# The adaptive modulation of a two-block kernel moved to TensorE, with its loads and those of x begun together

## The chip, the cores and the metric

One core of a Trainium2 chip runs the whole program. The metric is the device time of one execution in microseconds (us), as the median of the runs shown. All data is float32.

## The reference, cut to what matters

The function takes x (256 tokens of 1024 features) through two transformer blocks. The first one scales and shifts its normed input, and gates its branches, by six vectors that come from one vector c:

```python
mod = silu(c) @ w_ada + b_ada                        # (1, 1024) @ (1024, 6144)
sh1, sc1, g1, sh2, sc2, g2 = split(mod, 6)
u = rmsnorm(h, norm1_w) * (1.0 + sc1) + sh1
proj = u @ w_in                                      # hq, hf, hi, hg, aq, ak, av
...                                                  # gated recurrence (hgrn2) and differential attention
h = h + g1 * (mix @ w_out)
u = rmsnorm(h, norm2_w) * (1.0 + sc2) + sh2
h = h + g2 * ((silu(u @ w_gate) * (u @ w_up)) @ w_down)
```

The second block (gated linear attention, retention, a mixture of 32 experts with two per token, final norms) follows and has no part in the change.

## The kernel before, in words

Everything is one hand-scheduled program. Each engine has its own function (`tensor`, `scalar`, `vector`, `gpsimd`, `sync`) which is one long list of instructions in a fixed order; semaphores tie them together.

**Matrix products.** A product with 1024 input features and 512 output features (a `Gemm`, called hf, hq, aq, ak, av, hv, hg, wo0, ...) is cut into four units of two 128-feature chunks. The float32 weights of a unit are split into a high and a low half, ScalarE writing the high one (L846) and VectorE the low one (L1224), into a ring of three units (`WHL`). The activations are split in the same way into `XH` and `XL`. TensorE (L505) adds up three products for each chunk: high by high, low by high, high by low. A Gemm hands over control twice, after its second and after its fourth unit; such a half is called a half-product below.

**Weights.** SyncE issues all weight loads in one order into a ring of six slots of 1 MB, and waits before each until the slot is free. The modulation's matrix w_ada has twelve column blocks of 512 (ada0 to ada11), each of two loads (rows 0 to 511 and 512 to 1023). The order is ada0 to ada3, hf, hq, aq, ada4, ada5, ak, ada6, ada7, av, ada8, ada9, hv, hg, wo0, wo1, fg0, fu0, fg1, ada10, ada11, and so on. A slot that held a product's weights is free when VectorE has split them; one that held a block of w_ada, when TensorE has summed it.

**The modulation.** For block n, VectorE (`weigh`, L1264 to L1277) multiplies the rows 0 to 639 with silu(c), which lies as a column of 128 by 8 numbers, and adds them into a 128 x 512 accumulator: one instruction on L1273 and four on L1276. ScalarE (`weigh`, L924) scales the other three chunks of 128 rows in place. For blocks 4 to 11, GpSimd (L1918, L1920) adds those three into one. TensorE (`ada_sum`, L472) then sums over the partitions: for each 128 columns of the block a matmul with the accumulator as the stationary operand and a matrix of ones as the moving one, and one more for every other part (three for blocks 0 to 3, one for blocks 4 to 11). VectorE (`modulation`, L1281) adds b_ada and writes four columns of `modc`. Blocks 0 and 1 are sh1, 2 and 3 are sc1, and the first product needs these four; blocks 4 to 9 are used later, 10 and 11 last.

**The start.** ScalarE and SyncE issue the loads of fourteen small parameter rows, SyncE that of x before its share. SyncE waits until all of these have landed (L2006 to L2008) and only then issues the loads of w_ada. TensorE waits for all rows, turns them (L687), and then turns x chunk by chunk (L694); ScalarE and VectorE copy the chunks to `hT`. ScalarE computes silu(c) (L1074), later the squares (L904) that TensorE sums (L456) and of which ScalarE takes the root (L912). When four blocks of the modulation are there (`scl`, L1632), VectorE computes some small constants, both engines split the first two units of hf (`split_to(2)`, L1086 and L1656), and only then x is normed, shifted and split (L1258, L900, L1246).

**The woven stage.** From the product aq on, each engine's list is woven from lanes: after each half-product (a turn, numbered from 0), every live lane goes one step on. The lanes are the modulation's blocks 4 to 9, the gated recurrence (`gated`: TensorE's scores L532, VectorE's masks L1343, the differences L1307 and L1310, ScalarE's exponentials L935, VectorE's products L1323, GpSimd's products L1939) and from turn 4 the differential attention (`diff`: scores L593, then on VectorE L1372 to L1392). In VectorE's list the modulation's lane comes first: in each turn it ends block n, weighs block n+1, and then goes to the masks. Blocks 10 and 11 are woven into the gated feed-forward products (fg and fu).

Later stages: products of the second block, and the experts, whose weights stream in through ten more slots; there TensorE (L792) works with 64 stationary columns, two experts side by side in the two halves of the array.

## Time and profile before

| | us |
|---|---|
| median of 3 runs | 1417.17 (1416.83 to 1417.25) |
| the profiled execution | 1415.92 |
| its span, first to last instruction | 1414.1 |
| TensorE busy with matmuls | 1274.7 |
| VectorE busy | 656.2 |
| ScalarE busy | 484.3 |
| GpSimd busy | 84.2 |

Busy time counts an instruction from its start to its end; matmuls overlap, and a float32 matmul stands in the profile as two records. The granted clock of TensorE has two levels, 1.2 and 2.4 GHz, and its mean is 0.96 of the upper one. "q" behind an engine's name is its sequencer, where DMA issues stand. An arrow with a name in brackets says what ended the idle time ahead of an instruction.

### The profile page before, as it was taken

To read this page: it belongs to the slowest core of one execution; us is meant where nothing else is said; L and a number is where in the kernel's file an instruction comes from. 1 tells how busy PE (TensorE), PEld (TensorE's weight loads), DVE (VectorE), ACT (ScalarE), POOL (GpSimd) and SP (SyncE) were. 2 spreads that over 40 slices of the span, in tenths; PEclk is the share of its full clock that TensorE was granted. 3 is DMA by queue.
4 is the path that set the end of the run, shared out by engine and by line. 5 is a ranking of instruction groups with operands and counts; after the bars stand their busy time and mean duration, and the time that the engine had idled before them with its cause. 6 is when DMAs were issued, how large, how long until landed. Compare 5 with 4: busy or idle time off the path is not lost. (4 is left out here: it accounts for less than half of the span.)

```text
span 1414.1 us, 18306 instructions
## 1 busy us (share of the span) xinstructions
PE 1274.7 (90%) x7863; PEld 961.1 (68%) x7863; DVE 656.2 (46%) x978; ACT 484.3 (34%) x711; POOL 84.2 (6%) x73
## 2 busy tenths in 40 slices
PE   4778487899999899979999999779999999999996
PEld 4777376899999889868999999533443443434432
DVE  3678867674455668458654566541111102101111
ACT  3543354544444464534654544411010110001101
POOL 2023300010000112002020000000000000000000
PEclk9999797999999999989999999889999999999998
DMA  7826441358545343435344555759999999999993
GB/s 274 285 90 239 178 179 60 120 190 285 181 164 166 133 149 125 144 119 179 116 145 162 181 177 183 271 201 422 421 422 421 420 421 422 421 421 421 422 421 145
DMA packets 102164, 349.84 MB, mean 247 GB/s; under 512 B 5857, under 2 KB 9217, under 8 KB 77505
## 3 DMA queue, kind: packets, MB, share of 16 engines
q1 hardware_dynamic: 100654, 345.56, 64.6%
q0 software_dynamic: 1168, 2.99, 0.7%
q8 instruction: 63, 1.03, 0.3%
q14 instruction: 21, 0.16, 0.0%
q10 hardware_dynamic: 258, 0.10, 0.0%
HBM read 347.57 MB, written 1.05 MB: 247 GB/s over the span
## 5 line engine op out<-in xcount | busy, mean ns | idle before, releaser
L505 PE MATMUL bank<-XH,WHL 128*128 128x256 f32 x2928 | 546.9, 288 | 24.8 <-issue 9.1
L505 PEld LDWEIGHTS bank<-XH,WHL 128*128 128x128 f32 x2928 | 468.0, 195 | 28.9 <-issue 20.3
L505 PE MATMUL bank<-XL,WHL 128*128 128x256 f32 x1464 | 418.4, 286 | 0.0
L1224 DVE TENSOR_TENSOR WHL<-weights,WHL 128x1024 fp32r<-128x1024 f32 x223 | 279.0, 1268 | 201.2 <-ACT WHL L846 200.8
L846 ACT ACTIVATE WHL<-weights 128x1024 fp32r<-128x1024 f32 x223 | 232.0, 1055 | 209.2 <-PE bank L505 208.6
L505 PEld LDWEIGHTS bank<-XL,WHL 128*128 128x128 f32 x1464 | 286.2, 195 | 0.2
L505 PE MATMUL bank<-WHL,XH 128*128 128x512 f32 x320 | 105.8, 405 | 12.6 <-DVE WHL L1224 12.6
L1893 DVE TENSOR_TENSOR chainm<-bank,chainm 128x512 f32<-128x512 f32 x16 | 11.1, 692 | 171.9 <-PE bank L792 171.9
L792 PE MATMUL bank<-weights,arena 128*64 128x512 f32 x384 | 84.5, 592 | 0.0
L792 PE MATMUL bank<-arena 128*64 128x512 f32 x384 | 84.4, 592 | 0.0
L505 PEld LDWEIGHTS bank<-WHL,XH 128*128 128x128 f32 x320 | 62.1, 194 | 29.6 <-DVE WHL L1224 15.1
L1901 DVE COPY yo<-bank 128x512 f32<-128x512 f32 x16 | 11.1, 691 | 142.7 <-PE bank L827 142.7
L792 PEld LDWEIGHTS bank<-arena 128*64 128x64 f32 x384 | 27.6, 137 | 54.8 <-issue 54.8
L792 PEld LDWEIGHTS bank<-weights,arena 128*64 128x64 f32 x384 | 27.5, 137 | 54.6 <-issue 54.6
L505 PE MATMUL bank<-WHL,XL 128*128 128x512 f32 x160 | 63.9, 400 | 0.0
L668 PE MATMUL bank<-arena 128*128 128x256 f32 x256 | 58.9, 389 | 4.3 <-DVE arena L1602 4.3
L681 PE MATMUL bank<-yo,arena 128*128 128x512 f32 x128 | 57.7, 593 | 0.8 <-DVE yo L1901 0.8
L668 PEld LDWEIGHTS bank<-arena 128*128 128x128 f32 x256 | 49.5, 196 | 11.6 <-DVE arena L1602 4.5
L792 PE MATMUL bank<-late_weights,arena 128*64 128x512 f32 x256 | 56.3, 592 | 0.0
L1210 ACT ACTIVATE yo<-bank 128x512 f32<-128x512 f32 x16 | 9.6, 597 | 122.2 <-PE bank L827 122.2
L1276 DVE SCALAR_TENSOR_TENSOR arena<-weights,small,arena 128x512 f32<-128x512 f32 x48 | 48.0, 1001 | 2.5
L1612 DVE COPY arena<-bank 128x512 f32<-128x512 f32 x16 | 11.1, 691 | 77.2 <-PE bank L668 77.2
(309 smaller groups left out, 1252.7 us busy)
## 6 DMA issues: line engine op xcount, KB each, us to landing
weights<-in_w_in SPq DMA_DIRECT2D x58, 1024.0 KB, 5.1
weights<-in_w_ada SPq DMA_DIRECT2D x24, 1024.0 KB, 7.3
weights<-in_expert_w_gate SPq DMA_DIRECT2D x24, 1024.0 KB, 14.3
weights<-in_expert_w_up SPq DMA_DIRECT2D x24, 1024.0 KB, 15.5
arena<-in_expert_w_up SPq DMA_DIRECT2D x24, 1024.0 KB, 17.8
arena<-in_expert_w_down SPq DMA_DIRECT2D x24, 1024.0 KB, 20.1
weights<-in_expert_w_down SPq DMA_DIRECT2D x24, 1024.0 KB, 20.6
arena<-in_expert_w_gate SPq DMA_DIRECT2D x24, 1024.0 KB, 16.4
```

What stands on the lines that cost most here:

```text
L505: ins = e.matmul(o, l, r, start=first, skip_group_check=True, stop=g.part == g.parts - 1 and k == g.kc - 1 and n == 2)
L668: ins = e.matmul(bank[b][:, kk * T:(kk + 1) * T], utok[:, j, k * P:(k + 1) * P], pick[:, j, :], start=j == 0, stop=j == TT - 1)
L681: e.matmul(bank[b][:, :], wpT[p % 2][:, j * P:(j + 1) * P], yo[p % 2][:, n * 512:(n + 1) * 512], start=p == 0, stop=p == NPAIR - 1, skip_g ...
L792: ins = e.matmul(bank[b][64 * s_:64 * s_ + 64, :], xg[:, k, p % 2 * P + 64 * s_:p % 2 * P + 64 * s_ + 64], moe_weights(x, 4, HID)[:, kk, : ...
L846: e.activation(unit_halves(U)[0], unit_weights(g, u), ACT.Copy).then_inc(S.w_hi, 1)
L1210: e.activation(yo[p % 2][:, 512:1024], bank[7][:, :], ACT.Copy).then_inc(S.m_ya, 1)
L1224: e.tensor_tensor(lo, unit_weights(g, u), hi, ALU.subtract).then_inc(S.w_lo, 1)
L1276: e.scalar_tensor_tensor(out=m, in0=x, scalar=cT[:, k:k + 1], in1=m, op0=ALU.mult, op1=ALU.add).then_inc(S.ada_v, 1)
L1612: e.tensor_copy(xg[:, 2 * q:2 * q + 2, :], bank[5][:, :].rearrange("p (k s) -> p k s", k=2)).then_inc(S.m_xv, 1)
L1893: e.tensor_tensor(hp[p % 2], bank[5][:, :], hp[p % 2], ALU.mult).then_inc(S.m_h2, 1)
L1901: e.tensor_copy(yo[p % 2][:, 0:512], bank[6][:, :]).then_inc(S.m_yv, 1)
```

## The change

TensorE now computes the modulation by itself. ScalarE writes silu(c) 32 times side by side (`c32`, 128 x 8 x 32). For block n, `ada_sum` issues eight matmuls with 32 columns of `c32` as the stationary operand and 512 columns of w_ada as the moving one; chunk q of each load goes to the partitions 32q to 32q+31 of one PSUM bank, so the eight form four groups of array columns with two matmuls each. ScalarE copies the bank to a row buffer (`ada_row`). `ada_turn` issues four matmuls with 128 columns of that buffer as the stationary operand and the column `fold` (one at partitions 0, 32, 64 and 96, zero elsewhere) as the moving one, which adds the four groups and turns the result into four columns. VectorE adds b_ada as before. The weighing on VectorE and ScalarE and the additions on GpSimd are gone. A slot of w_ada is free after `ada_sum`.

In the start, TensorE turns x first and the rows after it; SyncE issues two rows (b_ada and c), x and at once the first six loads of w_ada, and waits for nothing ahead of them; ScalarE issues the other twelve rows. The small constants and the lambda of the differential attention move ahead or between. VectorE multiplies x by the reciprocal root while the modulation is still being computed; with the modulation there, ScalarE forms `XH` of chunk 0 from it directly, then splits two units of hf, then forms the other chunks.

In the woven stage, `ada_sum` comes in turns 0 to 5, `ada_turn` in the same turn behind the recurrence's scores; in VectorE's list the modulation comes behind the recurrence. Blocks 10 and 11 are summed at turns 4 and 5 of their stage, and turned at 5 and 6.

```diff
@@ tensor
             def ada_sum(n):
                 b = 6 + n % 2
-                parts = [in_slot(f"ada{n}", 1, 4, 512)[:, k, :] for k in range(1, 4)]
-                rows = [macc[n % 2]] + (parts if n < 4 else parts[:1])
                 clear(b)
-                w.wait_ge(S.ada_v, 5 * (n + 1))
-                w.wait_ge(S.ada_a, 3 * (n + 1))
-                if n >= 4:
-                    w.wait_ge(S.ada_o, 2 * (n - 3))
+                w.wait_ge(S.cT, 1)
+                for r in range(2):
+                    w.wait_ge(*landed(f"ada{n}", r))
+                    for q in range(4):
+                        ins = e.matmul(bank[b][32 * q:32 * q + 32, :], c32[:, 4 * r + q, :],
+                                       in_slot(f"ada{n}", r, 4, 512)[:, q, :], start=r == 0, stop=r == 1)
+                ins.then_inc(S.ada_p, 1)
+
+            def ada_turn(n):
+                b = 6 + n % 2
+                w.wait_ge(S.consts, 5)
+                w.wait_ge(S.ada_a, n + 1)
                 for c in range(4):
-                    for i, x in enumerate(rows):
-                        ins = e.matmul(bank[b][:, c * P:(c + 1) * P], x[:, c * P:(c + 1) * P], ones[:, :],
-                                       start=i == 0, stop=i == len(rows) - 1)
+                    ins = e.matmul(bank[b][:, c:c + 1], mrow[n % 2][:, c * P:(c + 1) * P], fold[:, :], start=True,
+                                   stop=True)
                 ins.then_inc(S.ada_p, 1)
                 free[b] = (S.mod, n + 1)
...
-            w.wait_ge(S.d_rows, 14 * 16)
             w.wait_ge(S.d_ident, 16)
-            e.transpose(bank[4][:, 0:P], prow, ident[:, :]).then_inc(S.rows_T, 1)
...
             for k in range(KC):
...
+            w.wait_ge(S.d_rows, 14 * 16)
+            e.transpose(bank[0][:, 0:P], prow, ident[:, :]).then_inc(S.rows_T, 1)
...
             weave([gemm(n) for n in ("aq", "ak", "av", "hv", "hg", "wo0")],
-                  (0, ada(range(4, 10))),
-                  (-1, gated(HG, [(S.hb, 1), by["hq"].freed[1]], by["hv"].freed[1])), (4, diff()))
+                  (0, ada(ada_sum, range(4, 10))),
+                  (-1, gated(HG, [(S.hb, 1), by["hq"].freed[1]], by["hv"].freed[1])),
+                  (0, ada(ada_turn, range(4, 10))), (4, diff()))
@@ scalar
-            def weigh(n):
-                w.wait_ge(S.cT, 1)
-                w.wait_ge(*landed(f"ada{n}", 1))
-                for k in range(5, KC):
-                    x = in_slot(f"ada{n}", 1, 4, 512)[:, k - 4, :]
-                    e.activation(x, x, ACT.Copy, scale=cT[:, k:k + 1]).then_inc(S.ada_a, 1)
+            def ada_row(n):
+                w.wait_ge(S.ada_p, 2 * n + 1)
+                e.activation(mrow[n % 2], bank[6 + n % 2][:, :], ACT.Copy).then_inc(S.ada_a, 1)
...
+            for k in range(KC):
+                e.activation(XH[:, k, :], scratch[:, k, :], ACT.Identity, bias=modc[:, k:k + 1],
+                             scale=scl[:, k:k + 1]).then_inc(S.x_hi, 1)
+                if k == 0:
+                    split_to(2)
@@ vector
-            def weigh(n):
...
+            for half in range(2):
+                ks = slice(4 * half, 4 * half + 4)
+                e.tensor_tensor(scratch[:, ks, :], hT[:, ks, :], rstd[:, :].unsqueeze(1).broadcast_to([P, 4, T]),
+                                ALU.mult).then_inc(S.xn, 1)
...
+            for k in range(KC):
+                e.tensor_scalar(xmod[:, k, :], scratch[:, k, :], scl[:, k:k + 1], modc[:, k:k + 1], ALU.mult,
+                                ALU.add).then_inc(S.xn, 1)
+                w.wait_ge(S.xn, 3 + k)
+                split_x(k, k, xmod[:, k, :])
+                if k == 0:
+                    split_to(2)
...
-                  (0, ada(range(4, 10))), (-1, gated(HG, [(S.hb, 1), by["hq"].freed[1]])), (4, diff()))
+                  (-1, gated(HG, [(S.hb, 1), by["hq"].freed[1]])), (0, ada(range(4, 10))), (4, diff()))
@@ gpsimd
-            weave([(x for x in range(2)) for _ in range(6)],
-                  (0, ada(range(4, 10))), (-1, gated(HG, [])))
+            run(gated(HG, []))
@@ sync
-            e.dma_start(xtok, a["x"][0].rearrange("(i p) d -> p i d", p=P)).then_inc(S.d_x, 16)
             for to, src in row_loads(False):
                 e.dma_start(to, src).then_inc(S.d_rows, 16)
-            w.wait_ge(S.d_rows, 14 * 16)
-            w.wait_ge(S.d_x, 16)
-            w.wait_ge(S.d_ident, 16)
+            e.dma_start(xtok, a["x"][0].rearrange("(i p) d -> p i d", p=P)).then_inc(S.d_x, 16)
...
-                        free[s] = (S.ada_p, n + 1)
+                        free[s] = (S.ada_p, 2 * n + 1)
```

## Rows read from the trace of the kernel before

**Rows 1.** The page: span, and busy time (share) of each engine.

```profile
span 1414.1 us, 18306 instructions
PE 1274.7 (90%) x7863; PEld 961.1 (68%) x7863; DVE 656.2 (46%) x978; ACT 484.3 (34%) x711; POOL 84.2 (6%) x73
```

**Rows 2.** Busy times by stage: length, PE, PEld, DVE, ACT, POOL, clock, DMA share, GB/s.

```profile
0.00:52.30 52.30, 24.65 (x163) 22.73 (x163) 23.99 (x53) 19.74 (x37) 8.96 (x18) 0.96 0.86 302
...
85.50:185.80 100.30, 70.31 (x462) 63.26 (x461) 81.96 (x116) 36.96 (x60) 29.99 (x20) 0.88 0.46 158
...
269.40:910.00 640.60, 615.74 (x4536) 588.74 (x4536) 385.99 (x458) 310.39 (x408) 43.42 (x35) 0.98 0.50 165
910.00:1414.00 504.00, 469.80 (x2056) 199.93 (x2056) 86.96 (x239) 54.46 (x98) 0.00 (x0) 0.97 0.93 387
```

**Rows 3.** Timeline of the start: start, us taken, engine, line, operation, [idle before].

```profile
8.83 21.96 SPq L2025 DMA_DIRECT2D weights<-in_w_ada  x8
8.86 0.47 PE L687 MATMUL bank<-ident,arena 128*128 128x128 f32 x1 [8.86 <-DMA arena<-in_c]
9.12 3.62 PE L694 MATMUL bank<-ident,arena 128*128 128x128 f32 x16
14.15 0.48 DVE L1273 TENSOR_SCALAR arena<-weights,small 128x512 f32<-128x512 f32 x1 [0.95 <-DMA weights<-in_w_ada]
18.81 1.28 ACT L908 ACT_TABLE_LOAD   x1
20.76 5.52 PE L456 MATMUL bank<-arena,ones 128*128 128x256 f32 x16 [8.01 <-ACT arena L904]
38.98 1.95 ACT L924 ACTIVATE weights<-weights,small 128x512 f32<-128x512 f32 x3 [8.52 <-DMA weights<-in_w_ada]
45.12 0.17 DVE L1632 SCALAR_TENSOR_TENSOR scl<-modc,pcol 128x8 f32<-128x8 f32 x1
47.19 1.98 ACT L846 ACTIVATE WHL<-weights 128x1024 fp32r<-128x1024 f32 x2
47.69 0.38 PE L702 MATMUL bank<-lams,ones 1*128 1x1 f32 x2 [2.80 <-DVE lams L1653]
48.26 2.36 DVE L1224 TENSOR_TENSOR WHL<-weights,WHL 128x1024 fp32r<-128x1024 f32 x2
52.34 0.55 PE L505 MATMUL bank<-XH,WHL 128*128 128x256 f32 x1 [4.28 <-DVE XL L1246]
```

**Rows 4.** Timeline of VectorE in the woven stage: turn 2, and from turn 4 on.

```profile
119.44 1.45 DVE L1273 TENSOR_SCALAR arena<-weights,small 128x512 f32<-128x512 f32 x1
120.92 4.10 DVE L1276 SCALAR_TENSOR_TENSOR arena<-weights,small,arena 128x512 f32<-128x512 f32 x4
124.94 1.33 DVE L1343 COPY_PREDICATED arena<-masks,bank 128x512 f32<-128x512 uint32 x2
...
128.57 0.69 DVE L1323 TENSOR_TENSOR arena<-arena 128x512 f32<-128x512 f32 x1 [1.12 <-ACT arena L935]
...
155.18 0.55 DVE L1372 SCALAR_TENSOR_TENSOR arena<-arena,bank 128x384 f32<-128x384 f32 x1
...
161.47 2.35 DVE L1224 TENSOR_TENSOR WHL<-weights,WHL 128x1024 fp32r<-128x1024 f32 x2
...
184.91 0.74 DVE L1343 COPY_PREDICATED arena<-masks,bank 128x512 f32<-128x512 uint32 x1 [0.73 <-PE bank L532]
```

**Rows 5.** TensorE in the woven stage: scores in the timeline; one half-product (busy time of L505).

```profile
94.16 3.75 PE L532 MATMUL bank<-arena 128*128 128x128 f32 x16 [6.67 <-DVE arena L1343]
...
106.06 1.95 PE L532 MATMUL bank<-arena 128*128 128x128 f32 x16
...
107.70:113.80 6.10, 5.99 (x48) 5.82 (x48) 1.00 0.92 335
```

**Rows 6.** Timeline of TensorE with the experts: 64 stationary columns, and 128.

```profile
944.19 1.51 PE L792 MATMUL bank<-weights,arena 128*64 128x512 f32 x6
...
982.91 1.45 PE L681 MATMUL bank<-yo,arena 128*128 128x512 f32 x3
```

More of the change, by code:

```diff
@@ L152, in build @@
         scratch = Region(ARENA - 1024 - KC * T).take([P, KC, T])
-        macc = [Region(ARENA - 1024 + 512 * i).take([P, 512]) for i in range(2)]
+        mrow = [Region(ARENA - 1024 + 512 * i).take([P, 512]) for i in range(2)]
+        xmod = Region(P).take([P, KC, T])
         b1 = Region()
@@ L1085, in scalar @@
             e.activation(lams[:, 2:4], lams[:, 0:2], ACT.Exp).then_inc(S.lam_a, 1)
-            split_to(2)
-            norm_split(0, 0, 0)
+            for n in range(1, 4):
+                ada_row(n)
+            w.wait_ge(S.scl, 1)
+            w.wait_ge(S.xn, 2)
+            for k in range(KC):
[3 more added lines that the diff above has]
+                    split_to(2)
             run(gemm("hf", to_features(hf, func=ACT.Sigmoid)))
```

117 lines of the change are left out of this document (50 added, 67 removed).

## The prediction

> **What bounds the kernel now.** I read the page first: TensorE is busy for 90% of the span, VectorE for 46% [rows 1]. That is an average, so the next view is the busy time by stage [rows 2]. From 269 to 910 us TensorE is busy for 616 of 641 us: it is the bound there, and what leaves VectorE is worth nothing. From 910 us on the experts' weights stream at 387 GB/s with the DMA engines 93% busy: transfers are the bound, and the stage keeps its length wherever it begins. Two stages are left. In the start (0 to 52.3 us) TensorE is busy for less than half of the time, so a chain of waits sets it. In the woven stage (85.5 to 185.8) VectorE is busy for 82 of 100 us and TensorE for 70. Since nothing behind 269 us waits for a clock time of its own, what these two stages gain arrives at the end in full.
>
> The timeline of the start [rows 3] shows the chain: no load of w_ada is issued before 8.83 us; the first lands at 14.15; TensorE's norm sums run from 20.76 to 26.3; the last piece of block 3 arrives only at 38.98, as slots are freed late; scl stands at 45.12, and the first product at 52.34. Of the last 7.2 us, 4.3 go to splitting two units of hf (1.98 and 2.36 [rows 3]), ahead of the shift of x.
>
> The timeline of VectorE in the woven stage [rows 4] shows what sets that one: in each turn it weighs a block for 5.5 us (119.44 to 124.94) before it comes to the masks, which the scores wait for (6.67 us of idle TensorE at the first [rows 5]).
>
> **The start, step by step.** x is third on its queue in place of first. Before, it had landed by 8.86 us, behind it eight rows; I take 7 us, and 9 as the late bound. TensorE turns it in 3.6 us [rows 3] and then the rows: 10.9. ScalarE's thirteen small loads must have landed by then; if they lag behind the stream of weights, each us late is a us lost (bounds 0 and 4; I take 0.3). Copying the rows and widening silu(c) take 0.7 us, two table loads 1.28 each [rows 3], of which one hides in part, and the squares start TensorE's norm sums at about 14.5; they take 5.5 as now and end at 20.0 in place of 26.3.
>
> Then four blocks in a chain. Each is: sum, ScalarE's copy, fold. No row shows four column groups. The nearest is the experts' matmul in two groups: six records, two abreast, take 1.51 us, where three of full width take 1.45 [rows 6]; so a record of 512 columns costs 0.43 us, and a second group costs nothing. The sum has sixteen records. Four abreast it takes 4 x 0.43 + 0.2 = 1.9 us; two abreast 3.6; one at a time 7.0. I take 1.9, since from one group to two no time is added, and keep the others as rivals. The fold is eight records with one moving column; the one such matmul takes 0.38 us for two records with the tail [rows 3], so four take 1.0 (bounds 0.8 and 1.5). The copy of 128x512 I put at 0.7 with its handoffs. A block is 3.7 us, four are 14.8, and the wait for lambda inside the second adds 0.8: 35.6, with the bias and scl 36.0, in place of 45.1.
>
> Do the loads keep up? A piece of 1 MB needs 2.7 us at the 387 GB/s of a full stream [rows 2] (the eight pieces now need 38.98 - 14.15 us only because of the slots). Issued from 2 us on, six have landed by about 24; the last two are issued when block 0 is summed, at 22, and land at 27 and 30. Block 3 is summed at 32, so this is close, but covered. The waits that SyncE gains come one block earlier than now.
>
> Behind scl now come only chunk 0's high part (0.5), one high half (1.0) and one low half (1.2): 2.9 us with handoffs in place of 7.2. First product: 38.9 in place of 52.3. Of these 13.4 us I take back 0.8, as VectorE forms the other seven chunks behind the two splits and is late with hf's third unit. **Gain of the start: 12.6 us** (bounds 8 and 16).
>
> **The woven stage.** VectorE loses 5.5 us in each of six turns; 33 us is the upper bound. What is late next is TensorE. Its turn is a half-product of 6.0, the sum 1.9 (as now: the old one had sixteen records of 128 columns, as the scores), the scores 1.95 [rows 5] and the fold 1.0, less overlaps 10.7 us. VectorE's turn is then masks 1.3, differences 1.3, the wait for ScalarE's exponential 1.12, products 0.7 [rows 4], and two low halves 2.4: seven us, so it waits for TensorE. ScalarE's copy stands in the shadow of the scores, but it is now ahead of the exponential on ScalarE's list, and waits for TensorE; the exponential is needed only after the masks, 2 us later, so nothing is queued up behind it. GpSimd has only its own products left.
>
> From the same instant, 85.5 us: turn 0 (sum, two scores, fold) ends at 92.2, turns 1 to 3 at 124.3. Turn 4's scores start at 132.0; masks, exponential and products end at 137.4; the attention's step on VectorE takes 6.3 (155.18 to 161.47 [rows 4]) and ends at 144.6. Turn 5 repeats this: splits 2.4, masks to products 5.3, step 6.3, splits 2.4, so turn 6's masks start at 161.4, where now they start at 184.91 [rows 4]. That is 23.5 us. Going from full width to narrow matmuls and back may cost a tenth of a us each time, and other handoffs as much; I take 2 off. **Gain: 21.5 us** (bounds 12 and 28, the latter where TensorE idles less and keeps the upper clock; in this stage its mean is 0.88 [rows 2]).
>
> **Blocks 10 and 11** lie where TensorE is the bound: the sum costs what the old one did, the fold is added: 2 x 1.1. **Loss: 2.2 us.** VectorE's 11 us there are worth nothing.
>
> **Sum.** 12.6 + 21.5 - 2.2 = 31.9 off the profiled 1415.92: 1384.0. The median is 1.25 above that execution: 1385.2, which I round to 1385.
>
> **The rivals.**
>
> *Two groups abreast at most.* The sum costs 3.6 to 4.0 us in place of 1.9, and all twelve sums lie on the path: 20 to 25 us given back, 1405 to 1410. For: only two groups are shown. Against: in rows 6 the first two records of different groups start as a pair; were records held to program order, with the two of one matmul in sequence, six of them would need 1.51 + 0.43 us. The Trainium skill (TensorE: Matmul & The Clock Gate, Part 3) says that matmuls stay in strict program order; by that the sum is 8 x 0.43 + 0.6 = 4.0 us and the time about 1410. The trace disagrees for two groups, and shows nothing for four. Chance 0.10.
>
> *The groups don't overlap at all.* Each sum costs 7.0 us, 5.1 more than forecast, twelve times: 61 us, so 1446, slower by 29. Its place is `ada_sum`; it decides from 4.6 us a sum on, where the 32 us are used up. Against it stand the experts' matmuls. Chance 0.04.
>
> *The woven stage doesn't give what VectorE gets back.* If ScalarE, now tied to TensorE twice a turn, or loads that arrive late hold the turns at 12 to 13 us, only some 5 us come of that stage: 1401. For: TensorE's turn grows by the fold. Against: ScalarE is busy for 37 of 100 us there [rows 2]. Chance 0.10.
>
> *The loads are not earlier in effect.* If the small rows land late behind the weights, silu(c) and all four blocks wait: from 13 us late on the start gives nothing and the time is 1398; with 32 us late nothing is left and the time is that of before. Chance 0.05, of which 0.01 for no change.
>
> **How the numbers follow.** The forecast with its bounds (1374 to 1396) has 0.71. The first rival 0.10, the third 0.10, the fourth 0.05, the slower one 0.04. The range reaches from 1374 to 1409, which leaves out the slower case and the tails. About 0.2% is what a measurement of this kernel can tell from no change (1414.3 to 1420.0). Faster 0.95, same 0.01, slower 0.04.
>
> **What would show it right or wrong.** In the profile of the changed kernel: loads of w_ada from about 2 us; norm sums over at 20; four groups of sixteen narrow records of 1.9 us each (this first: 3.6 or 7.0 would be the first two rivals); scl at 36; the first product at 39; in the woven stage scores every 10.7 us, VectorE busy below 65%, masks waiting for TensorE; from the norm sums of the second norm on the same lengths as now. The forecast is wrong if the first product comes after 45 us, or if the time from the first recurrence scores to the first attention scores hasn't shrunk.

## The result, and the profile after

The changed kernel takes 1383.41 us (median of 4 runs, 1382.53 to 1388.14), beside 1417.11 for the one before on the same chip: a ratio of 0.9769 (95% interval 0.9758 to 0.978), 33.7 us less. The forecast was 1385, with a range of 1374 to 1409. Executions of this kernel differ more among themselves than those of the one before. The profiled execution took 1382.53 us, with a span of 1380.7. Line numbers below are those of the changed kernel: L471 is the sum, L934 ScalarE's copy, L481 the fold, L541 the scores, L602 the attention scores, L514 the products.

The page, span and busy time, against [rows 1]:

```profile
span 1380.7 us, 18262 instructions
PE 1277.5 (93%) x7895; PEld 946.7 (69%) x7895; DVE 605.0 (44%) x925; ACT 470.9 (34%) x688; POOL 61.0 (4%) x57
```

TensorE has as much to do as before, and VectorE 51 us less: the gain is idle time of TensorE. Where it went is seen in the busy times by stage, cut at the same instructions as in [rows 2]; only the woven stage ends a little earlier, at turn 6's scores, and its line for the kernel before comes first:

```profile
85.54:183.82 98.28, 68.29 (x446) 61.24 (x444) 81.02 (x114) 36.92 (x60) 29.95 (x20) 0.88 0.46 161
```

```profile
0.00:38.30 38.30, 21.62 (x132) 13.44 (x132) 10.89 (x37) 15.77 (x29) 8.98 (x18) 0.97 0.98 356
...
72.35:148.53 76.18, 70.88 (x493) 56.06 (x493) 50.16 (x85) 29.63 (x48) 12.83 (x8) 0.93 0.69 249
...
236.00:876.60 640.60, 615.04 (x4554) 585.78 (x4554) 377.34 (x450) 307.63 (x404) 37.28 (x31) 0.99 0.50 166
876.60:1380.70 504.10, 471.07 (x2056) 200.62 (x2055) 85.81 (x236) 54.47 (x98) 0.00 (x0) 0.97 0.93 385
```

The start is 38.3 us long in place of 52.3. The woven stage, from the end of aq's first half-product to turn 6's scores, is 76.2 in place of 98.3, with TensorE busy for 93% of it. VectorE is busy for 66% of it; the prediction had named below 65% as a sign. From 236 us on, both stretches have the lengths of before to 0.1 us. What was gained in front arrives at the end in full; that the first of the two stretches keeps its length, though it now holds two folds more, has a reason of its own (see the account of blocks 10 and 11).

The timeline of the start (start, us taken, engine, line, operation, idle before), against [rows 3]:

```profile
2.08 5.67 SPq L2025 DMA_DIRECT2D weights<-in_w_ada  x4
...
8.73 0.28 DVE L1625 TENSOR_TENSOR lamrow<-lamrow 1x128 f32<-1x128 f32 x1 [7.24 <-DMA lamrow<-in_diff_lambda_k]
...
9.70 1.54 PE L700 MATMUL bank<-ident,arena 128*128 128x128 f32 x6 [0.40 <-DVE hT L1630]
...
14.93 5.51 PE L458 MATMUL bank<-arena,ones 128*128 128x256 f32 x16 [3.47 <-ACT arena L917]
20.37 1.92 PE L471 MATMUL bank<-weights,c 128*32 128x512 f32 x16
...
27.68 1.92 PE L471 MATMUL bank<-weights,c 128*32 128x512 f32 x16
30.32 1.05 PE L481 MATMUL bank<-fold,arena 128*128 128x1 f32 x8 [0.72 <-ACT arena L934]
31.31 1.92 PE L471 MATMUL bank<-weights,c 128*32 128x512 f32 x16
...
35.23 0.17 DVE L1661 SCALAR_TENSOR_TENSOR scl<-modc,pcol 128x8 f32<-128x8 f32 x1
...
38.29 0.58 PE L514 MATMUL bank<-XH,WHL 128*128 128x256 f32 x1 [3.29 <-DVE WHL L1240]
```

The loads begin 6.7 us earlier. The sum takes 1.92 us for its sixteen records. A block is sum, 0.72 us of waiting for ScalarE's copy, and fold: 27.68 to 31.31, 3.63 us. One wait nobody had counted: VectorE, first in line with lambda's product, waits for a small row from GpSimd's queue, its first copies of x come late for it, and TensorE idles for 0.40 us between transposes (the last kernel below removes this wait, and meets the next one).

TensorE in the woven stage, against [rows 5]:

```profile
95.35 1.92 PE L471 MATMUL bank<-weights,c 128*32 128x512 f32 x16
97.20 2.05 PE L541 MATMUL bank<-arena 128*128 128x128 f32 x16
99.09 0.95 PE L481 MATMUL bank<-fold,arena 128*128 128x1 f32 x8
...
105.83 1.92 PE L471 MATMUL bank<-weights,c 128*32 128x512 f32 x16
...
123.64 0.94 PE L602 MATMUL bank<-arena 64*128 64x128 f32 x8 [2.92 <-DVE modc L1282]
...
139.19 2.07 PE L602 MATMUL bank<-arena 64*128 64x128 f32 x8 [2.36 <-ACT arena L981]
```

The turn shown is 10.48 us long (95.35 to 105.83) and holds no idle time of TensorE. Only at the attention scores does it still wait, 2.92 and 2.36 us. VectorE in the same turn, against [rows 4]:

```profile
98.40 0.73 DVE L1343 COPY_PREDICATED arena<-masks,bank 128x512 f32<-128x512 uint32 x1 [2.50 <-PE bank L541]
...
103.27 3.11 DVE L1240 TENSOR_TENSOR WHL<-weights,WHL 128x1024 fp32r<-128x1024 f32 x2 [0.19 <-ACT WHL L859]
108.88 0.73 DVE L1343 COPY_PREDICATED arena<-masks,bank 128x512 f32<-128x512 uint32 x1 [2.49 <-PE bank L541]
```

The roles are reversed: before, TensorE waited for the masks; now the masks wait 2.5 us for TensorE's scores.

### The profile page after: what moved, and what is told of

The parts are those of the page before. It is cut to its first block and busy times, and to the rows that moved or that the text cites. A ratio compares the mean times of both kernels' runs of the same rounds, so it can differ in the third digit from the quotient of the medians.

```text
span 1380.7 us, 18262 instructions
## 1 busy us (share of the span) xinstructions
PE 1277.5 (93%) x7895; PEld 946.7 (69%) x7895; DVE 605.0 (44%) x925; ACT 470.9 (34%) x688; POOL 61.0 (4%) x57
## 3 DMA queue, kind: packets, MB, share of 16 engines
HBM read 347.57 MB, written 1.05 MB: 253 GB/s over the span
## 5 line engine op out<-in xcount | busy, mean ns | idle before, releaser
L514 PE MATMUL bank<-XH,WHL 128*128 128x256 f32 x2928 | 547.2, 288 | 22.7 <-issue 9.1
L514 PEld LDWEIGHTS bank<-XH,WHL 128*128 128x128 f32 x2928 | 468.1, 195 | 28.5 <-issue 17.8
L514 PE MATMUL bank<-XL,WHL 128*128 128x256 f32 x1464 | 418.6, 286 | 0.0
L1240 DVE TENSOR_TENSOR WHL<-weights,WHL 128x1024 fp32r<-128x1024 f32 x223 | 279.8, 1270 | 209.4 <-ACT WHL L859 208.9
L514 PEld LDWEIGHTS bank<-XL,WHL 128*128 128x128 f32 x1464 | 286.1, 195 | 0.2
L514 PE MATMUL bank<-WHL,XH 128*128 128x512 f32 x320 | 106.0, 406 | 9.4 <-DVE WHL L1240 9.4
L514 PEld LDWEIGHTS bank<-WHL,XH 128*128 128x128 f32 x320 | 62.6, 196 | 26.4 <-DVE WHL L1240 11.7
L514 PE MATMUL bank<-WHL,XL 128*128 128x512 f32 x160 | 64.4, 403 | 0.0
L840 PE MATMUL bank<-weights,masks 128*64 128x512 f32 x192 | 43.0, 596 | 2.7 <-ACT masks L1220 2.7
L840 PE MATMUL bank<-arena,masks 128*64 128x512 f32 x192 | 42.8, 594 | 2.7 <-ACT masks L1220 2.7
## 6 DMA issues: line engine op xcount, KB each, us to landing
arena<-in_expert_w_down SPq DMA_DIRECT2D x24, 1024.0 KB, 20.4
```

The source lines that it names most:

```text
L514: ins = e.matmul(o, l, r, start=first, skip_group_check=True, stop=g.part == g.parts - 1 and k == g.kc - 1 and n == 2)
L840: ins = e.matmul(bank[6 + n][64 * s_:64 * s_ + 64, :], hpT[p % 2][:, k, 64 * s_:64 * s_ + 64], moe_weights(x, 2, D)[:, kk, n * 512:(n + 1) ...
L1240: e.tensor_tensor(lo, unit_weights(g, u), hi, ALU.subtract).then_inc(S.w_lo, 1)
```

## The experiments

The time of a run differs by up to 8 us between executions of one kernel (1374.66 to 1382.91 in e10), so most verdicts rest on lengths of stages in the profile. They are cut at three points that every kernel has: the first product, the first product of the feed-forward stage, and the end. The two columns in the middle tell how long TensorE was busy in the woven part and its mean granted clock there: between kernels with the same sums (the changed one, e3 to e9 and e12), more busy time is a lower clock, and the rest of the length is idle time. "Time" is that of the profiled execution; e1, e2, e4 and e8 ran only once. All but the clock are in us.

| kernel | first product at | from it to feed-forward | TensorE busy in it | clock in it | from there to the end | time |
|---|---|---|---|---|---|---|
| before | 52.34 | 217.1 | 164.5 | 0.90 | 1144.7 | 1415.92 |
| changed | 38.29 | 197.7 | 169.8 | 0.91 | 1144.7 | 1382.53 |
| e1 two groups | 45.23 | 208.2 | 180.3 | 0.92 | 1148.0 | 1403.26 |
| e2 one group | 58.73 | 223.0 | 194.7 | 0.94 | 1156.8 | 1440.45 |
| e3 waits back | 42.60 | 201.6 | 173.6 | 0.89 | 1144.9 | 1390.75 |
| e4 VectorE work, woven | 39.12 | 208.9 | 173.8 | 0.88 | 1144.6 | 1394.53 |
| e5 VectorE work, feed-forward | 38.14 | 195.5 | 167.3 | 0.92 | 1146.5 | 1382.03 |
| e6 VectorE and GpSimd work | 38.76 | 218.8 | 175.0 | 0.87 | 1144.5 | 1404.07 |
| e7 GpSimd work alone | 38.97 | 198.7 | 170.6 | 0.91 | 1144.7 | 1384.34 |
| e8 splits first | 39.01 | 191.9 | 163.8 | 0.94 | 1146.5 | 1379.26 |
| e9 order of the start | 40.12 | 197.7 | 169.8 | 0.91 | 1144.7 | 1384.38 |
| e10 blocks 10 and 11 in the gap | 39.02 | 198.3 | 174.0 | 0.91 | 1141.4 | 1380.52 |
| e11 all | 38.01 | 201.4 | 177.1 | 0.89 | 1141.4 | 1382.69 |
| e12 unchanged | 39.32 | 198.6 | 170.7 | 0.91 | 1144.9 | 1384.67 |

Of the last stretch one thing has to be known before its lengths are compared. In the second block's gated linear attention TensorE sums squares for the norm of each of four heads, four records a head (called the head sums below). In some executions the granted clock falls there, and those of the last two heads take 2.04 us each in place of 1.10, 1.9 us together. The third head in the kernel before, in the changed one, and in e5 and e8:

```profile
598.16 2.04 PE L559 MATMUL bank<-arena,ones 128*128 128x256 f32 x4 [1.18 <-ACT arena L952]
```

```profile
567.43 1.10 PE L568 MATMUL bank<-arena,ones 128*128 128x256 f32 x4 [1.17 <-ACT arena L962]
```

```profile
564.26 2.05 PE L570 MATMUL bank<-arena,ones 128*128 128x256 f32 x4 [1.17 <-ACT arena L964]
```

```profile
561.49 2.04 PE L568 MATMUL bank<-arena,ones 128*128 128x256 f32 x4 [1.17 <-ACT arena L962]
```

It falls so in the kernel before, in e2, e5, e8, e10 and e11, and not in the changed kernel, e1, e3, e4, e6, e7, e9 and e12.

### What a sum costs: two groups and one

```
-        c32 = sb("c32", [P, KC, 32])
+        c32 = sb("c32", [P, KC, 64])
...
-                        ins = e.matmul(bank[b][32 * q:32 * q + 32, :], c32[:, 4 * r + q, :],
-                                       in_slot(f"ada{n}", r, 4, 512)[:, q, :], start=r == 0, stop=r == 1)
+                        ins = e.matmul(bank[b][64 * (q % 2):64 * (q % 2) + 64, :], c32[:, 4 * r + q, :],
+                                       in_slot(f"ada{n}", r, 4, 512)[:, q, :], start=r == 0 and q < 2,
+                                       stop=r == 1 and q >= 2)
```

The column `fold` has its ones where the groups begin. The second kernel has 128 for 64 and one group. Expected:

> The changed kernel (1383.4 us) with c held in 64 equal columns instead of 32, so that a sum goes to two column groups of 64 and only two of its records can run abreast; the copies, the fold and all waits stay. Theory of the forecast (a record of 512 columns costs 0.43 us, groups run abreast without a price, and all twelve sums lie on the path): a sum takes 3.6 us in place of 1.92, 12 x 1.7 = 20 us more, 1404 us; somewhat less, about 1400, if TensorE's waits in the woven stage (2.9 and 2.4 us at the attention scores) take up part of it. Rival A, the two records of each float32 matmul stay in sequence and only the next matmul overlaps: 4.0 us a sum, 1408. Rival B, the number of groups has nothing to do with it and the sum is short for another reason (something in narrow stationary operands): still about 1.9 us a sum and 1383.

> The changed kernel with c held in all 128 columns, so that a sum uses the whole array one record after the other. Theory of the forecast: a sum takes 16 x 0.43 = 7.0 us, 5.1 us more, twelve times 61 us: 1444 us, slower than the kernel before (1417). If the woven stage had room beside TensorE (a sum hidden behind another wait), the six sums there would give less and the time would be about 1420. Rival, the groups buy nothing: 1383.

Measured: 1403.26 and 1440.45 us, one run each. TensorE's timeline with two groups, and then with one:

```profile
20.47 3.65 PE L471 MATMUL bank<-weights,c 128*64 128x512 f32 x16
```

```profile
20.46 7.03 PE L471 MATMUL bank<-weights,c 128*128 128x512 f32 x16
```

1.92, 3.65 and 7.03 us with four, two and one group, for the same sixteen records: the groups run abreast without a price, and nothing else about the narrow operand makes the sum short (that rival falls, and with 3.65 in place of 4.0 us so does the other). By these three times a record of 512 columns takes its group 0.43 us. In the table each stage holds the count of sums that the forecast gave it. With one group the start is 20.4 us longer (4 x 5.11), and what follows the woven stage 12.1 (2 x 5.11 is 10.2, and the head sums lost 1.6 us of clock in this execution). The woven stage is 25.3 longer and not 30.7. Not that the waits ahead of the attention scores took up the rest, as the expectation had guessed: they are as long as before (2.91 and 2.36 us). The busy times of that stretch tell (PE busy is the second number, granted clock the third from the end):

```profile
58.70:281.70 223.00, 194.65 (x1156) 158.74 (x1157) 130.82 (x204) 93.09 (x159) 14.74 (x8) 0.94 0.44 150
```

and the changed kernel's:

```profile
38.30:236.00 197.70, 169.78 (x1157) 146.84 (x1157) 130.99 (x204) 93.07 (x159) 14.76 (x8) 0.91 0.52 180
```

TensorE is busy for 24.9 us more, not 30.7, and idle as long: the same number of instructions, at a granted clock of 0.94 in place of 0.91. That TensorE, busier with its sums, kept more of its clock is possible but not shown: e8 has the same 0.94 with the sums of the changed kernel. With one group the kernel is slower than before (1416.57 on that chip), as the slower rival had it; with two it keeps 13 of the 33.7 us.

### What the woven stage's gain is made of

Four kernels with additional idle work (e5, the fourth, has VectorE's chain in the feed-forward stage); nothing of the computation is changed. The core of the edits: VectorE's chain (e4 to e6), where it stands in the woven stage, and GpSimd's two additions (e6 and e7):

```
+            def extra(count):
+                for _ in range(count):
+                    for k in range(5):
+                        w.wait_ge(S.idle, done[0])
...
+                            e.scalar_tensor_tensor(out=idle[:, :], in0=idle[:, :], scalar=pcol[:, 0:1], in1=idle[:, :],
+                                                   op0=ALU.mult, op1=ALU.mult).then_inc(S.idle, 1)
...
-                  (-1, gated(HG, [(S.hb, 1), by["hq"].freed[1]])), (0, ada(range(4, 10))), (4, diff()))
+                  (0, extra(6)), (-1, gated(HG, [(S.hb, 1), by["hq"].freed[1]])), (0, ada(range(4, 10))), (4, diff()))
...
+                    for k in range(2):
+                        w.wait_ge(S.idlep, 1 + 2 * t + k)
+                        e.tensor_tensor(idlep[:, :], idlep[:, :], idlep[:, :], ALU.add).then_inc(S.idlep, 1)
```

> The changed kernel with additional work on VectorE: in each of the six turns of the woven stage that had a weighing before the change, ahead of the masks, five instructions of 128x512 in a chain on a tile of their own (5.5 us, as the old weighing had), with no load, no sum and no other engine behind them. Nothing of the computation is changed. Theory of the forecast (the stage got shorter because VectorE is rid of 5.5 us a turn ahead of the masks): the turn grows from 10.5 to about 13 to 14 us and the two turns with attention by the full 5.5; 18 to 22 us come back, 1402 to 1405. Rival, the gain came from GpSimd's and ScalarE's shares of the old weighing, which held TensorE's sum: TensorE sets the turn now, VectorE has 3 us to spare, and 0 to 6 us come back, 1383 to 1389.

Measured: 1394.53 us in one run, the stretch 11.2 us longer. Both theories missed. Of the 11.2, TensorE is idle for 7.2 more; for the other 4.0 it is busy with the same instructions at a clock of 0.88 in place of 0.91. My five instructions took 3.5 us and not the 5.5 that I had ascribed to them: alone, each of the four last takes 0.75 (view of that tile; duration in ns as min/median/max):

```profile
L1301 DVE SCALAR_TENSOR_TENSOR idle_work<-idle_work,pcol x24: 750/752/755, 77.4 to 146.8; 128x512 f32<-128x512 f32 x24
```

In the kernel before, the same form took 750 to 1839 ns in the woven stage. The four in turn 2 together took 4.10 us [rows 4], and in turn 1 5.00. The timeline of GpSimd in the kernel before shows what lies beside them:

```profile
119.19 1.41 POOL L1918 TENSOR_TENSOR weights<-weights 128x512 f32<-128x512 f32 x1 [1.96 <-ACT weights L924]
120.68 1.36 POOL L1920 TENSOR_TENSOR weights<-weights 128x512 f32<-128x512 f32 x1
```

VectorE's two long ones are the first, at 119.44 (1.45), and the one from 120.92 on: each beside one of GpSimd's additions. From this came a new theory and two more runs.

> The woven stage with additional work on VectorE (five instructions, 3.5 us a turn, which alone gave 1394.5 us and lengthened the stage by 9.8) and, beside it, on GpSimd: two additions of 128x512 a turn as the old weighing had, begun when VectorE's first is done, on tiles of their own; nothing of the computation is changed. Theory 1, new: GpSimd's additions slow VectorE. In the trace of the kernel before, VectorE's weighing instructions take 0.75 us alone and 1.66 where one of GpSimd's additions lies beside them, two of five in every turn; that is what makes the old weighing 5.5 us and not 3.5. Then two of VectorE's five take 1.6 us here too, the turn grows from 10.5 to about 12.4, and the stage by some 10 to 12 us more: 1404 to 1407. Rival, the long instructions of before were long for another reason (reading the slot while a transfer writes its neighbour, or the slot itself): GpSimd's part costs nothing, 1394 to 1396.

> The changed kernel with GpSimd's two additions of 128x512 alone in each of six turns of the woven stage, begun when ScalarE has copied the block's row, and nothing more on VectorE; nothing of the computation is changed. By the theory that each addition adds 0.9 us to a VectorE instruction beside it: 1.8 us a turn, which VectorE's idle time (about 3 us a turn) takes up in four turns, and which shows at most in the two turns with attention, where VectorE's work is in line: 0 to 4 us, 1383 to 1388. Rival, GpSimd's work holds the stage in its own right (its products of the recurrence come later because of the additions): one to two us in every turn, 6 to 12 us, 1390 to 1395.

Measured: 1404.3 us (1404.07 and 1404.57) with both, 1385.35 (1384.34 and 1386.36) with GpSimd's part alone. VectorE waits for nothing of GpSimd's in this kernel, and yet its four now range up to 1.63 us, and in one turn take 4.65 in place of 3.1:

```profile
L1302 DVE SCALAR_TENSOR_TENSOR idle_work<-idle_work,pcol x24: 751/1081/1633, 78.2 to 156.9; 128x512 f32<-128x512 f32 x24
...
108.06 4.65 DVE L1302 SCALAR_TENSOR_TENSOR idle_work<-idle_work,pcol 128x512 f32<-128x512 f32 x4
...
108.11 2.48 POOL L1954 TENSOR_TENSOR idle_work_pool<-idle_work_pool 128x512 f32<-128x512 f32 x2 [2.69 <-DVE idle_work L1300]
```

With both the stretch is 218.8 us, the kernel before had 217.1: the old length is back, without a load, a sum or a wait of the old weighing. Of the 21 us, 11.2 came with VectorE's own 3.5 us a turn and 9.9 with GpSimd's additions: 8.7 of these are idle time of TensorE, 1.2 its lower clock, and VectorE's chain is 1.54 us longer in each turn (9.2 in six). GpSimd's alone cost nothing that shows (198.7 us, and the unchanged kernel had 197.7 and 198.6), since VectorE then has time to spare. The attention scores show the same: TensorE waits for the first of them 2.92 us in the changed kernel, 6.33 with VectorE's chain and 9.85 with both.

```profile
142.28 1.66 PE L605 MATMUL bank<-arena 64*128 64x128 f32 x8 [9.85 <-DVE modc L1285]
```

The Trainium skill (SBUF — State Buffer, Who interferes with whom) says that VectorE and GpSimd share a pair of ports under an exclusive lock, and that a VectorE instruction with two inputs in SBUF contends with a GpSimd instruction that reads SBUF, the later one waiting. The trace agrees that the two meet: VectorE's 0.75 us become 1.63 beside an addition. Which of them waits it doesn't tell: the long instruction stands 0.05 us ahead of the addition (108.06 and 108.11), and the pair of additions takes 2.48 us here and 2.16 in most turns without VectorE's chain. In the kernel before, the chain's first instruction, with one input of that size, was long beside an addition too (1.45 us [rows 4], 0.47 alone); no run tests that one by itself.

> The changed kernel with the same additional instructions of VectorE as the run before (five of 128x512 in a chain, 3.5 us, six times, nothing of the computation changed), but in the first six half-products of the feed-forward stage, where TensorE is busy without a break. Theory of the forecast (there TensorE is the bound and what leaves or enters VectorE is worth nothing): no change, 1383 to 1386 us. Rival, VectorE's low halves of the weights are made with no time to spare and each chain makes TensorE wait: up to 6 x 3.5 = 21 us, 1404.

Measured: 1383.39 us (1382.03 and 1384.76). The same 3.5 us of VectorE, six times, in the feed-forward stage cost nothing that shows against 1383.41. From there to the end the profiled execution needs 1146.5 us in place of 1144.7, but that is the clock in the head sums: e8 has the same 1146.5 without any additional work. The feed-forward products themselves, up to the second block's first, take 210.16 us here and 210.36 in the changed kernel. The rival falls.

### What the early loads are worth

```
+            w.wait_ge(S.d_rows, 14 * 16)
+            w.wait_ge(S.d_x, 16)
+            w.wait_ge(S.d_ident, 16)
             for name in order:
```

> The changed kernel with the three waits of SyncE (the small rows, x, the identity) put back ahead of the loads of w_ada, so that these begin at about 8 us as before the change and not at 2.1; everything else stays. Theory 1, pieces land at 2.7 us each and block 3 is what counts: six pieces land by 6 x 2.7 + some 14 = about 28 us in place of 24.97, the last two are issued when block 0 is summed (22.3) and land at about 31 and 33.5 in place of 27.7 and 30.4, block 3 is summed at about 33.7 in place of 31.3: 2 to 2.5 us more, 1385.5 to 1386. Rival, the early issue carries most of the start's 13 us: the whole chain moves by the 6 us that the loads come later, 1389. A third way: nothing at all (1383.4), if TensorE's chain of sum, copy and fold hides all of it.

Measured: 1388.76 us (1386.15 to 1390.75, 4 runs): 5.3 more than the 1383.41, 4.2 more than the 1384.53 of the unchanged kernel on another chip, so between the two theories. The loads begin at 9.2 us. TensorE's timeline:

```profile
31.65 1.07 PE L471 MATMUL bank<-weights,c 128*32 128x512 f32 x8
34.79 1.94 PE L471 MATMUL bank<-weights,c 128*32 128x512 f32 x8 [2.07 <-DMA weights<-in_w_ada]
37.44 1.87 PE L481 MATMUL bank<-fold,arena 128*128 128x1 f32 x8 [0.72 <-ACT arena L934]
42.60 0.58 PE L514 MATMUL bank<-XH,WHL 128*128 128x256 f32 x1 [3.29 <-DVE WHL L1240]
```

Theory 1's wait is there (2.07 us for block 3's second piece), and with it the clock (granted clock 1.00 up to 32.7 us, 0.50 behind the wait): the half-sum takes 1.94 us where the one ahead of the wait takes 1.07, the fold 1.87 in place of 1.05. The first product comes 4.3 us later: 2.1 of waiting and 1.7 of clock make 3.8 of it, and 0.35 lie ahead of the first sum, since the norm sums end at 20.72 in place of 20.37. The 4.3 us are all that this section shows of the 14.0 gained at the first product; the other shares (x and its norm sums 5.9 us earlier, shorter blocks, less behind scl) are read from the timelines and not tested one by one. The following stretch is 3.9 us longer in this execution, and that is clock too: TensorE is busy there for 3.85 us more with the same instructions, at 0.89 in place of 0.91:

```profile
42.60:244.10 201.50, 173.63 (x1156) 150.44 (x1156) 130.98 (x204) 93.02 (x159) 14.74 (x8) 0.89 0.50 174
```

Whether the late start lowered it there, or that execution was one of the slower ones (four went from 1386.15 to 1390.75), the runs don't tell.

### One order at the start of the products

The third edit put hf's two splits ahead of the shift of x's chunk 0, on ScalarE and VectorE:

```
+            split_to(2)
             w.wait_ge(S.scl, 1)
...
-                if k == 0:
-                    split_to(2)
```

> The changed kernel with the splits of hf's first two units put back ahead of the shift of x's chunk 0 on ScalarE and VectorE, as before the change. By the forecast's term (7.2 us behind scl became 2.9 by this order) the first product would come up to 4.3 us later. By what the trace shows now (hf's first piece lands at 34.5, before scl at 35.2, so that one split fits ahead of scl): ScalarE makes two high halves to 36.6 and chunk 0 to 37.1, VectorE two low halves to 38.0 and chunk 0's low part to 39.0, first product at about 39.2 in place of 38.3, 0.9 us later, and from there the following units are ready earlier. Time between 1383.0 and 1384.5 by this, 1387 to 1388 by the forecast's term.

The first product comes at 39.01, 0.7 us later, close to the 39.2 expected from the trace; the forecast's 4.3 us were not there to be had by this order. In the kernel before, VectorE didn't go from scl to the splits: it had 3.1 us of small constants and lambda first, which the change moved elsewhere. The first and the last of them, and then its splits in this run:

```profile
45.20 0.15 DVE L1635 TENSOR_TENSOR small<-pcol 128x4 f32<-128x4 f32 x1
...
48.10 0.16 DVE L1655 COPY small<-bank 128x1 f32<-128x1 f32 x1 [0.47 <-PE bank L702]
```

```profile
35.77 2.36 DVE L1239 TENSOR_TENSOR WHL<-weights,WHL 128x1024 fp32r<-128x1024 f32 x2 [0.38 <-ACT WHL L859]
```

Scl stands at 35.22 here, and the splits follow 0.55 us later, not 3.14 (45.12 to 48.26 [rows 3]). The transfer of hf ends at about the same time, 34.5.

The time, 1379.26, is one run and below what either theory gave. Its second stretch is 5.8 us shorter than the changed kernel's, and TensorE is busy there for 5.9 us less with the same instructions, at a granted clock of 0.94:

```profile
39.00:230.90 191.90, 163.84 (x1156) 141.78 (x1157) 129.49 (x203) 91.58 (x156) 14.76 (x8) 0.94 0.53 184
```

Whether this order favours the clock, or the run was one of its better ones, is open.

### Can more be had?

Two edits and both together, five runs of each, beside five of the changed kernel itself. Both together has a third, small edit: VectorE's work for lambda behind its copies of x. The order of the start:

```
-            for n in range(4):
-                ada_sum(n)
-                if n == 1:
+            for step, n in ((ada_sum, 0), (ada_sum, 1), (ada_turn, 0), (ada_sum, 2), (ada_turn, 1), (ada_turn, 2),
+                            (ada_sum, 3), (ada_turn, 3)):
+                if step is ada_turn and n == 2:
```

and the two last blocks in the gap of the second norm:

```
-                  "ada8", "ada9", "hv", "hg", "wo0", "wo1", "fg0", "fu0", "fg1", "ada10", "ada11"]
+                  "ada8", "ada9", "hv", "hg", "wo0", "wo1", "ada10", "ada11"]
...
             norm_sums(1)
+            ada_sum(10)
+            ada_sum(11)
```

The folds of these two then come at the second and third turn.

> The changed kernel with TensorE's order in the start changed: sums 0 and 1, fold 0, sum 2, folds 1 and 2, then sum 3 and fold 3, so that no copy by ScalarE stands between a sum and the next. In the changed kernel a block is a chain of sum, copy and fold (3.63 us each from 20.4 us on), scl stands at 35.2, and the last piece of w_ada has landed at 30.4. Theory 1, the chain sets the start and the transfers are nearly as long: block 3's second half is summed as soon as its piece lands (30.4 to 31.5), copy to 32.2, fold to 33.2, scl at 33.5, hf's first piece lands at about 33.5 because its slot is freed 1.8 us earlier, first product at 36.6 to 37: 1.3 to 1.7 us less than the unchanged kernel beside it. Rival, the transfers already set it: 0 to 0.4 us. The third, a clock that falls in the new waits: 1 us more.

> The changed kernel with blocks 10 and 11 loaded ahead of the feed-forward stage's weights and summed right behind the sums of the second norm, where TensorE stands idle for 4.1 us, in place of the fifth and sixth half-product. Theory 1 (a sum lies where TensorE is the bound and costs its 1.92 us, an idle stretch takes it for nothing): 2 x 1.9 = 3.8 us less than the unchanged kernel beside it, and up to 1.7 us more if TensorE's clock no longer falls after the gap (in the changed kernel the granted clock is low from 236.9 us for 3.4 us). Rival, the ring of six slots: four of them are held until the sums, the weights of the first products come later and TensorE waits for their splits: no gain, or up to 3 us more.

> Both of the runs before in one kernel, and VectorE's product and sum for lambda moved behind its copies of x, where they no longer hold these until a small transfer lands (0.4 us in TensorE's transposes). If the parts add up: 1.5 + 3.8 = 5.3 us less than the unchanged kernel beside it, 1378; the 0.4 us are hidden by then, since the last piece of w_ada sets the start. If each part is only worth what the transfers leave: 3 to 4 us less.

> The changed kernel as it is, beside the three runs before on the same chip, so that their differences of 1 to 5 us can be told from the spread of its own runs (1382.5 to 1388.1 so far): 1383.4 again, between 1382.5 and 1385 by any theory.

Measured, medians of five: unchanged 1384.53 (1384.14 to 1384.67), order of the start 1383.99 (1382.76 to 1385.76), gap 1379.41 (1374.66 to 1382.91), all 1380.4 (1378.23 to 1382.98); before 1417.34.

**The gap** gives 5.1 us by the medians: 0.9729 of the time before (0.971 to 0.9748). All its runs lie below all of the unchanged kernel's; against the kernel with both edits (0.9722 to 0.975) it is not told apart. Its timeline of TensorE:

```profile
229.53 3.69 PE L460 MATMUL bank<-arena,ones 128*128 128x256 f32 x16 [1.12 <-ACT arena L920]
233.15 3.64 PE L473 MATMUL bank<-weights,c 128*32 128x512 f32 x32
237.33 0.36 PE L516 MATMUL bank<-XH,WHL 128*128 128x256 f32 x1 [0.54 <-issue]
```

The sums fill what was 4.11 us of idle time, the products begin as far behind the norm sums as before (7.80 us), and from there to the end 3.5 us are saved. Up to the second block's first product it is 4.9 us (205.4 in place of 210.35), of 3.8 for the sums and up to 1.7 for the clock that were expected; 1.9 us are then lost in the head sums, whose clock fell in e10 and e11 and not in e12. The clock behind the gap is better. The same 11.8 us from the norm sums on in the gap kernel, and then in the unchanged one (granted clock is the third number from the end):

```profile
229.50:241.30 11.80, 11.23 (x81) 7.89 (x82) 9.67 (x22) 6.92 (x17) 0.00 (x0) 1.00 0.43 148
```

```profile
230.10:241.90 11.80, 7.65 (x39) 6.94 (x40) 9.68 (x22) 6.91 (x17) 0.00 (x0) 0.89 0.23 85
```

In each of the twelve kernels with the gap unfilled the clock falls for some time near the first feed-forward product; in the two with the sums in it, it doesn't. The rival (slots held too long) did not come: the products wait for no split.

**The order of the start** gives 0.5 us, inside the spread; in the profiled execution the first product comes 0.8 us later than in the unchanged kernel beside it (40.12 and 39.32), where 1.3 to 1.7 us less were expected. TensorE in the run with both:

```profile
29.34 1.07 PE L473 MATMUL bank<-weights,c 128*32 128x512 f32 x8
31.88 1.06 PE L473 MATMUL bank<-weights,c 128*32 128x512 f32 x8 [1.47 <-DMA weights<-in_w_ada]
```

The chain of blocks now waits for the last piece of w_ada, 1.47 us here and 0.72 in the run with this order alone. There the clock fell as well, and not behind the wait but ahead of it, within the first half-sum:

```profile
30.13 1.45 PE L473 MATMUL bank<-weights,c 128*32 128x512 f32 x8
32.30 1.93 PE L473 MATMUL bank<-weights,c 128*32 128x512 f32 x8 [0.72 <-DMA weights<-in_w_ada]
```

So the transfers were nearly the bound already: the rival was nearer, helped by the third case, the clock. In the run with both, the first product is 1.3 us earlier than in the unchanged one beside it (38.01 and 39.32), but 1.07 of that lie ahead of the first sum, which starts at 20.33 and 21.40: the unchanged kernel's norm sums took 6.60 us in that execution, and those of the changed kernel's first profile 5.51. From the first sum to the first product it is 17.68 us and 17.92: the new order is worth 0.24 us, inside the rival's 0 to 0.4. The third edit brought nothing either. The transposes of x run through, but TensorE then waits for a small row:

```profile
11.49 0.47 PE L706 MATMUL bank<-ident,arena 128*128 128x128 f32 x1 [0.74 <-DMA arena<-in_ret_norm_w]
```

In the changed kernel this transpose stands at 11.04. The next stretch is 2.8 us longer than in the unchanged kernel (201.4 and 198.6) at a mean clock of 0.89 in place of 0.91. The medians give 4.1 us for both edits, where the parts would make 5.6; with spreads of 5 and 8 us that difference isn't shown.

## Why the prediction was right

The measured time lies 1.6 us below the forecast, and the mechanism was the one foretold. Two of its reasons were wrong where the size came out right, and two effects of the clock that it didn't have cancel.

- **The sum, 1.9 us.** 1.92, and with fewer groups 3.65 and 7.03 where the rivals had 3.6 and 7.0. The Trainium skill's rule (TensorE: Matmul & The Clock Gate, Part 3), as the prediction applied it to the two records of each matmul, would have made 4.0 us of a sum and 1410 us of the time; the measurement decides against that reading.
- **The start, gain 12.6.** Norm sums end at 20.4 (forecast 20.0), blocks take 3.63 each (3.7), scl stands at 35.2 (36.0), the first product at 38.3 (38.9). The 0.8 us for the wait for lambda didn't come: its matmul at 26.04 fits between the sum and the fold, while ScalarE copies. 14.0 us are gained at the first product; at the end of aq's first half-product, 72.35 in place of 85.54, it is 13.2 (forecast 12.6, where 0.8 had been taken back).
- **"Do the loads keep up?"** Close, but covered, as the prediction said: the last piece of block 3 lands at 30.4, and its sum begins at 31.3; the changed order of the start then ran into them at once.
- **The 4.3 us behind scl.** The length, 3.1 us, was right (2.9), the reason was not: luck. The prediction added up two splits of two engines that overlap (47.19 to 50.6 us, 3.4 and not 4.3) and took them for what the new order saves; with the old order it is 3.8 us. Of the 4.1 us saved, 3.1 are VectorE's small constants and lambda, which had stood between scl and its splits and which the prediction's sum doesn't name.
- **The woven stage, gain 21.5.** From the first sum to turn 6's scores 22.1 us. The walk through the turns had slips of its own: 137.4 and a step of 6.3 make 143.7 and not 144.6, and the terms behind it are 0.4 us short of 161.4; added up as they stand they give 24.8 us in place of 23.5. The 2 us taken off for narrow matmuls and handoffs rest on no row, and no run shows them as such. The turn is 10.48 us (10.7), TensorE is the bound in it, ScalarE's copy holds nobody. The 5.5 us a turn were the right size, but they are not all VectorE's own work: by the runs with idle work 3.5 are, and 2 come from GpSimd's additions beside it. The change takes both away, so the sum held. Had it kept GpSimd's additions beside other work of VectorE, a forecast by VectorE's durations would have failed.
- **Blocks 10 and 11, loss 2.2.** By the start of feed-forward the lead is 33.43 us (269.42 and 235.99), and at the second block's first product it is 31.5 (477.82 and 446.35): a loss of 1.95. At the end the lead is 33.4 again. No step of the forecast gives that: 1.9 us of it are the head sums, at the lower clock in this execution of the kernel before and not in that of the changed one.
- **The sum of terms** is 31.9, measured 33.4 between the profiled executions. The terms themselves make 13.2 + 22.1 - 1.95 = 33.3, each a little better than forecast. The clock gave and took beside them: from turn 6's scores to feed-forward the changed kernel needs 1.86 us more (87.46 and 85.60), all of it busy time of TensorE with the same instructions (clock 0.88 and 0.90), and the head sums gave 1.9 back. That these two cancel is chance.

## What to carry to other kernels

A sum over few rows that VectorE weighs can go to TensorE with a narrow stationary operand in as many column groups as there are, at a cost divided by their number (measured for one, two and four); count the idle time that VectorE leaves TensorE, not VectorE's busy time. When an instruction of VectorE shows two durations for one shape, look at GpSimd's timeline beside it before calling it work. Once the idle time is gone from a stage, put the remaining sums where TensorE still idles: here the gap of a norm was worth more (5.1 us by the medians) than a shorter chain in front (0.5, inside the spread). And before a difference of 2 us between two profiles is called an effect, compare their TensorE busy times and clocks stage by stage: several of them here were the clock alone.

## What the runs showed of the hardware that was not expected

- Four column groups of 32 columns run fully abreast in float32: sixteen records of 512 columns in 1.92 us, where sixteen of full width take 7.03.
- Beside GpSimd's additions of 128x512, a VectorE instruction with two inputs in SBUF takes up to 1.63 us in place of 0.75.
- A wait of TensorE of 2.07 us on a transfer was followed by records at about half speed: half a sum 1.94 us in place of 1.07, a fold 1.87 in place of 1.05. In another run a wait of 1.47 us was not, and in a third the clock fell ahead of the wait. Filling 3.64 of 4.11 idle us with sums kept the granted clock of that stretch at 1.00 (0.89 without).
- The same instructions at the same place run at either clock level from one execution to the next: the last two head sums 1.10 us each or 2.04.
